# First loads asked for a stage ahead, modulation's weights in six loads, and row turning placed differently, in a two-layer diffusion trunk

## What is computed

```python
for i in range(DEPTH):                                  # 2 layers
    mod_l = split_cols(silu(c) @ w_mod[i] + b_mod[i])   # shift, scale, gate, twice
    mod_c = split_cols(silu(c_ctx) @ w_mod[i] + b_mod[i])
    a = modulate(rmsnorm(h, norm1_g[i]), ...)
    o = gla_mixer(...) if i == 0 else diff_mixer(...)   # mixer, ends in "@ w_out"
    h = h + gate * o
    f = modulate(rmsnorm(h, norm2_g[i]), ...)
    h = h + gate * peer_ffn(f, peer_wq[i], peer_subkeys[i], peer_u[i], peer_v[i])
return rmsnorm(h_lat, final_g)

def peer_ffn(h, wq, subkeys, u, v):
    q = (x @ wq).reshape(C, 8, 2, 128)                  # product keys
    s = einsum('chzd,zkd->chzk', q, subkeys)            # top 16 of 128, twice
    ...                                                 # top 16 of 256 pairs, softmax g
    act = gelu(einsum('cd,chkd->chk', x, u[idx]))       # rows of u, 16384 experts
    return einsum('chk,chkd->cd', g * act, v[idx])
```

## Time and profile before

| | us |
|---|---|
| median of 3 runs | 5217.56 (5213.93 to 5222.57) |
| the profiled execution | 5214.52 |
| its span | 5212.7 |

### The profile page before, as it was taken

The page is one execution under the profiler, slowest core; times in us unless marked ns, Lnnn a source line. Parts: engine busy times, 40 slices in busy tenths (PEclk is TensorE's granted clock), DMA queues, the critical chain, the costliest instruction groups (busy, mean ns, idle before and its releaser), DMA issues. The chain is left out here.

```text
span 5212.7 us, 54609 instructions
## 1 busy us (share of the span) xinstructions
PE 4361.0 (84%) x18847; PEld 2971.3 (57%) x18847; DVE 3454.1 (66%) x7226; ACT 1212.6 (23%) x2191; POOL 1825.8 (35%) x1652
## 2 busy tenths in 40 slices
PE   5799985793887799999999957886737777999997
PEld 4476764483555466666666625553433435666665
DVE  2256665468988877776777745675588775666665
ACT  0223321110343311111111112331212332222222
POOL 0021112022666655554555500000126774343441
PEclk9899978897999899999999979997868889999999
DMA  7577764612899999999999946667318999999995
GB/s 251 188 226 210 224 191 137 223 62 94 328 374 346 332 374 359 356 358 343 369 356 359 350 129 187 193 167 203 125 65 313 339 336 359 356 355 357 356 358 196
DMA packets 514294, 1407.95 MB, mean 270 GB/s; under 512 B 45661, under 2 KB 128605, under 8 KB 509183
## 3 DMA queue, kind: packets, MB, share of 16 engines
q1 hardware_dynamic: 329726, 733.60, 43.3%
q0 software_dynamic: 184320, 671.17, 34.0%
HBM read 1226.33 MB, written 178.26 MB: 269 GB/s over the span
## 5 line engine op out<-in xcount | busy, mean ns | idle before, releaser
L1623 POOL DMA_INDIRECT expert_rows<-u_rows,peer_arena x640 | 893.1, 1395 | 1311.3 <-DVE expert_rows L1897 1049.2
L1668 PE MATMUL ps<-part_arena,peer_part_arena 128*128 128x384 f32 (+1 forms) x4096 | 1034.7, 335 | 29.5 <-DVE peer_part_arena L1940 27.6
L1897 DVE SCALAR_TENSOR_TENSOR expert_rows<-expert_rows,mixer_in 128x1024 f32<-128x1024 f32 x640 | 759.9, 1220 | 125.0 <-DMA expert_rows<-u_rows,peer_arena 121.8
L1640 PE MATMUL ps<-expert_rows,peer_arena 128*128 128x512 f32 x1024 | 540.3, 680 | 329.8 <-DVE peer_arena L1905 327.5
L1630 POOL DMA_INDIRECT expert_rows<-in_peer_v,peer_arena x640 | 729.4, 1140 | 195.1 <-issue 186.0
L1668 PEld LDWEIGHTS ps<-part_arena,peer_part_arena 128*128 128x128 f32 x4096 | 698.4, 189 | 92.4 <-issue 77.6
L1677 PE MATMUL ps<-best,peer_arena 128*128 128x512 f32 x1540 | 685.3, 592 | 0.0
L1668 PE MATMUL ps<-mixer_in_parts,peer_part_arena 128*128 128x384 f32 (+1 forms) x2048 | 632.9, 309 | 0.0
L1640 PEld LDWEIGHTS ps<-expert_rows,peer_arena 128*128 128x128 f32 x1024 | 212.4, 217 | 602.4 <-issue 311.7
L1924 DVE SCALAR_TENSOR_TENSOR peer_arena<-expert_rows,peer_arena 128x1024 f32<-128x1024 f32 x381 | 489.4, 1285 | 30.5 <-DVE peer_arena L1924 2.3
L1450 POOL TENSOR_TENSOR part_arena<-peer_arena,part_arena 128x1024 fp32r<-128x1024 f32 x32 | 76.4, 2390 | 1077.8 <-ACT part_arena L1427 1077.8
(11 more groups left out here) (250 smaller groups left out, 6212.9 us busy)
## 6 DMA issues: line engine op xcount, KB each, us to landing
peer_arena<-in_peer_u SPq DMA_DIRECT2D x256, 512.0 KB
best<-in_peer_v SPq DMA_DIRECT2D x154, 512.0 KB
mixer_arena<-in_peer_u SPq DMA_DIRECT2D x296, 256.0 KB, 7.5
u_rows<-mixer_arena SPq DMA_DIRECT2D x148, 512.0 KB, 6.3
hidden<-in_peer_u SPq DMA_DIRECT2D x216, 256.0 KB, 6.3
u_rows<-hidden SPq DMA_DIRECT2D x108, 512.0 KB, 4.8
gates<-peer_arena SPq DMA_DIRECT2D x20, 2048.0 KB
peer_arena<-in_peer_v SPq DMA_DIRECT2D x52, 512.0 KB
```

What stands on the lines that cost most here:

```text
L1623: pool.indirect_dma_start(u_ring[:, k % U_SLOTS, :], None, u_table, bass.IndirectOffsetOnAxis(u_index[s][:, m:m + 1], 0)).then_inc(u_row_i ...
L1640: mm = pe.matmul(ps[:, 2 + half, :], diag[m % V_SLOTS], v_ring[:, m % V_SLOTS, half * 512:half * 512 + 512], start=m == 0, stop=m == PAIRS ...
L1668: mm = pe.matmul(ps[:, 6, 0:dense_tok], left[j % len(left)][:, c, :], right[:, c, :], start=at == 0, stop=at == len(todo) - 1)
L1897: dve.scalar_tensor_tensor(out=rows, in0=rows, scalar=1.0, in1=B.x[:, :, rows_at + s * P:rows_at + s * P + P], op0=ALU.mult, op1=ALU.mult, ...
```

## The change

1. Each mixer, project_out and product_keys has its first loads in a function `ahead`. The norm ahead of gla, attention and product_keys calls it at its beginning; gla and attention call project_out's on SyncE between their last heads, when the region that the weights go to is free. Their semaphores are kept (`B.kept`) and not cleared between the layers; the clears are worked out after all stages are made.
2. project_out has four weight slots instead of two, filled ahead; the loops of TensorE (project_out) and SyncE (product_keys) are written out.
3. Modulation has a buffer for all 16 tiles and asks for them in six loads (1, 1, 2, 4, 4, 4 tiles) at once, ahead of hidden, gains and identity, whose wait is now the stage's last step on SyncE.
4. Turning units: modulation 10 to 4, beginning of gla 6 to 12, project_out 0 14 to 16, beginning of attention 8 to 4, project_out 1 10 to 12. In gla the first four are turned one after each log gate, and SyncE's loads of head 1's weights stand after the sixth and the ninth `follow`. In attention the four come after VectorE's part of the prologue, and SyncE waits for the prologue's last unit and loads head 2's weights before the first `follow`.

```diff
-TURNED_EARLY = (10, 14)
-TURNED_LATE = 10
+TURN_MOD, TURN_GLA, TURN_ATT, TURN_OUT = 4, 12, 4, (16, 12)
+OUT_SLOTS = 4
...
+        B.start_loads = [(B.h, a["hidden"]), (small[:, 0:5 * C], a["gains"]), (B.ident[:, :], a["ident"])]
+        stages = [make(modulation)]
         for layer, segs in ((0, (CTX, LAT)), (1, (LAT,))):
+            project = make(project_out, a["gla_w_out"] if layer == 0 else a["diff_w_out"], segs[0][0], layer, segs)
+            mixer = make(gla if layer == 0 else attention, project["ahead"])
+            keys = make(product_keys, layer, segs)
+            stages += [make(norm, layer, B.gains[:, layer], 0, 1, (CTX, LAT), 0, mixer["ahead"]),
+                       mixer, project,
+                       make(norm, layer, B.gains[:, 2 + layer], 3, 4, segs, SPARSE_TILES[layer], keys["ahead"]),
+                       keys, make(peer, layer, segs)]
...
         @block.sync
         def _(sp):
-            sp.dma_start(B.h[:, :, :], a["hidden"]).then_inc(start_in, 16)
-            sp.dma_start(small[:, 0:5 * C], a["gains"]).then_inc(start_in, 16)
-            sp.dma_start(B.ident[:, :], a["ident"]).then_inc(start_in, 16)
-            sp.wait_ge(start_in, 48)
             run(sp, "sync")
...
 def modulation(B):
-    M = 4
-    loads = 2 * C // M
+    SIZES = (1, 1, 2, 4, 4, 4)
...
     def sync(sp):
         sp.dma_start(raw, B.a["cond"]).then_inc(cond_in, 16)
         sp.dma_start(B.mod_bias, B.a["b_mod"]).then_inc(cond_in, 16)
-        for n in range(2):
-            tiles.load(sp, n, n % 2)
+        for n, m in enumerate(SIZES):
+            at = slice(FIRST[n], FIRST[n] + m)
+            sp.dma_start(w[:, at].rearrange("p m c n -> p m (c n)"), B.a["w_mod"][at].rearrange("m p c n -> p m (c n)")
+                         ).then_inc(w_in[n], 16)
+        for to, at in B.start_loads:
+            sp.dma_start(to, at).then_inc(start_in, 16)
         turner.begin(sp)
...
     def tensor(pe):
-        pe.sem_inc(tiles.used, 2)
         pe.wait_ge(cond_ready, 1)
-        for n in range(loads):
-            tiles.multiply(pe, n, n % 2, n * M)
+        for m in range(2 * C):
+            if m in FIRST:
+                pe.wait_ge(w_in[FIRST.index(m)], 16)
+            for c in range(C):
+                mm = pe.matmul(out[:, m, :], w[:, m, c, :], B.cond[:, c, :], start=c == 0, stop=c == C - 1)
+        mm.then_inc(summed, 1)
...
+    def sync(sp):
+        if ahead:
+            ahead(sp)
...
     def sync(sp):
         turner.begin(sp)
         for m in range(2):
             mod.load(sp, m, m)
-        for n in range(BEFORE):
+        for n in range(6):
             turner.follow(sp, n)
         sp.wait_ge(u_mm, LAST_QKG + 1)
-        weights(1)
+        weights(sp, 1)
+        for n in range(6, 9):
+            turner.follow(sp, n)
         sp.wait_ge(u_mm, NU)
-        v_weights(1)
+        v_weights(sp, 1)
+        for n in range(9, BEFORE):
+            turner.follow(sp, n)
...
+            if h + 2 <= H:
+                sp.wait_ge(u_mm, NU * (h + 2))
             if h + 2 < H:
-                sp.wait_ge(u_mm, NU * (h + 2))
-                v_weights(h + 2)
+                v_weights(sp, h + 2)
+            if h + 2 == H:
+                for n in range(OUT_SLOTS):
+                    project_ahead(sp, n)
...
             if UNITS[u][0] == Z:
                 log_gates(0, 0, u)
-        for n in range(BEFORE):
+                turner.turn(dve, place(0, u) - 1)
+        for n in range(NZ, BEFORE):
             turner.turn(dve, n)
         heads(dve, head)
...
     def sync(sp):
         turner.begin(sp)
+        sp.wait_ge(u_mm, NP)
+        weights(sp, 2)
         for n in range(BEFORE):
             turner.follow(sp, n)
-        sp.wait_ge(u_mm, NP)
-        weights(2, 0)
...
+        prologue(unit)
         for n in range(BEFORE):
             turner.turn(dve, n)
-        prologue(unit)
         heads(dve, head)
```

205 lines of the change are left out of this document (108 added, 97 removed).

## The result

The changed kernel takes 5135.04 us (median of 4 runs, 5133.48 to 5138.93) against 5215.75 (4 runs, 5213.3 to 5222.57) of the kernel before: a ratio of 0.9844, 95% interval 0.9827 to 0.9861, faster by 1.6%. The forecast was 5139. The profiled execution has a span of 5134.5 us, 78.2 less than before.

The account below looks back on a forecast made before the run. Outside the TensorE-bound peer stages, the prediction took transfers, filled by turning units, as the main limit. Terms -40 - 8 + 6 - 9.5 - 33 + 6 = -78.5 took 5217.6 to 5139 us, range 5112 to 5172.

Parts of the forecast that it names:

- Modulation, -40: Modulation: four units instead of ten and six loads at once end it at 65 us; -40, between -33 and -45.
- gla, -8: Beginning of gla: loads ahead save 17.5 us, twelve units make VectorE late by 9; -8 remains.
- The bounds, +5 to -24: gla's beginning: +5 if holds leave the queue empty for 13 us, -24 if all twelve units fit under TensorE.
- The two holds: gla's beginning: stores of units 6 and 9 wait behind SyncE's waits for TensorE's twelfth and last unit; bound +5.
- project_out, +6 and +6: Both project_out stages, full of transfers: two units more, four weights fewer; +6 each, between +1 and +10.
- product_keys, -9.5: Both product_keys: first loads, 4.9 and 4.6 us, become hidden in the norm ahead; -9.5, between -6 and -10.
- attention, -33: Beginning of attention: the head begins at +60 instead of +88.9, and TensorE is a projection ahead; -33, between -27 and -38.
- Peer stages, 0: Peer stages: TensorE is busy throughout with transfers hidden under it, and the change leaves them alone; 0.
- (1): Rival: units are cheaper beside TensorE, gla's beginning hides all twelve and gains 24 instead of 8; 5123, chance 0.17.
- (2): Rival: moved units and SyncE's waits cost more, in gla, modulation, project_out and attention; 30 us more, 5169, chance 0.21.
- (3): Rival: loads ahead in gla, product_keys and attention are not early in effect; 36 us lost, 5175, chance 0.04.
- (4): Rival: TensorE's clock stays at 1.2 GHz from modulation through gla's beginning; 106 us more, 5245, chance 0.03.

Follow-up runs that it names:

- hid_first: Changed kernel with hidden, gains and identity asked for ahead of modulation's six weight loads, without a wait between; 5144.2 us.
- mod10: Changed kernel with layer 0's units placed as before, ten in modulation and six at gla's beginning; 5157.2 us.
- g_early: Changed kernel with gla's first two units turned on VectorE before the first log gate; 5135.3 us.
- a_early: Changed kernel with two of attention's four units turned and stored ahead of VectorE's part of the prologue and SyncE's wait for TensorE's fifth unit; 5124.2 us.
- no_ahead: Changed kernel with the first loads of gla, attention and product_keys asked for at the stage's own beginning, not in the norm ahead; 5177.1 us.
- heads5: Changed kernel with eight units fewer in the project_out stages (12 and 8) and five units per attention head instead of four; 5089.3 us.
- no_out_ahead: Changed kernel with each project_out's four first weights asked for at its own beginning, not in gla and attention; 5151.1 us.
- the repetition: The changed kernel measured again with no edit, in a later group of runs; 5138.9 us.
- g_early2: g_early with SyncE's loads of head 1's weights moved behind the ninth and twelfth unit's stores; 5123.3 us.

## Why the prediction was right, point by point

**The time.** 5139 against 5135.0, in a range of 5112 to 5172. The forecast's case held; the errors of its terms are +5 us in gla, -3 in project_out 1 and -3 in the norms. That they cancel to less than 1 us is luck.

**Modulation, -40: -40.4.** End foreseen at 65, measured 64.64, with the 256 records in one stretch of 54.75 us. The sum of bytes carried it: the window shows 324 GB/s, where 317 was taken. TensorE's end, at 60.25, was close behind, as the upper bound said, and hid_first shows the margin, 4 us. The forecast gave no split; mod10 gives it: nine tenths are the units.

**gla, -8: -2.9 in the first pair of profiles, none in the second.** The first product came at once, as foreseen (-17.5). The first k_d transpose slipped to +108.6, foreseen +107.5 (17.5 less the slip of 9 is 8.5, which the prediction wrote as 8). The step that failed is the sentence that put "all of head 0" behind it, as if it took as long as before: the way from that transpose to the forward part took 49.3 us instead of 44.5 (14.6 us of slip at the forward part, of which 9.8 stood at the transpose). The windows show where the 4.8 us are. Each cuts this way in two at the same instruction, 31 or 32 records behind its beginning and 203 ahead of its end, after first, then before:

```profile
208.62:218.20 9.58, 9.58 (x31) 8.37 (x32) 3.78 (x8) 4.93 (x8) 0.00 (x0) 0.50 1.05 298
218.30:257.80 39.50, 37.31 (x203) 30.30 (x201) 16.18 (x33) 15.55 (x26) 0.00 (x0) 0.89 1.02 313
```
```profile
257.60:262.60 5.00, 5.00 (x32) 4.62 (x32) 1.38 (x4) 4.52 (x7) 0.00 (x0) 1.00 0.36 81
262.60:302.00 39.40, 37.41 (x203) 30.39 (x201) 15.71 (x32) 15.96 (x28) 0.00 (x0) 0.89 1.04 319
```

Behind its wait of 17.21 us TensorE does in 9.58 us what took 5.00 before: its granted clock is 0.50, the lower level, 1.2 GHz, instead of 1.00. The remaining 203 records take the same time in both, with one wait of 2.2 us for a tile of w_mod against 2.0, so the full queue costs nothing more here. The prediction priced VectorE's delay, and not what TensorE's rest does to the work behind it. The other runs bear out that it goes with the rest: in the seven other profiles with this wait (16.8 to 18.9 us; g_early, a_early, no_ahead, hid_first, heads5, no_out_ahead and the repetition) the 16 records on w_mod right behind the transpose take 3.41 or 3.42 us, as here, and where the wait is missing (before, mod10, g_early2) 1.84 or 1.85. Taking the rest away didn't give the 4.8 us back, though: g_early2 needs 49.4 us for the same part, with two other stretches of lower clock inside it (0.57 from 193.7 to 197.7, 0.68 from 207.9 to 218.5) that no run here explains. The bounds, +5 to -24, held the term. The two holds that the bound of +5 priced (SyncE's waits between the stores) cost nothing in the changed kernel, and 15 us as soon as the units came earlier (g_early).

**project_out, +6 and +6: +6.6 and +3.0.** The mechanism was right (full queue, two units more, four weights less; no_out_ahead puts the weights at 12.2 us for the two, 15.2 foreseen). The size of the second was off by the rate that the profile of before happened to show, 293 GB/s against 310 after: 88 us at 310 are 27.3 MB, which at 293 would have been 93 us, +7.

**product_keys, -9.5: -9.6** with the norms ahead of them, -10.5 without. As foreseen.

**attention, -33: -32.3.** The head begins at +59.3 (foreseen +60), behind the wait of 17.44 us that was named; a_early shows the mechanism by taking it away.

**Peer stages, 0:** +1.8 and -1.2, inside what they move by themselves. The norms' 3 us less was not foreseen, and no run here explains it.

**The rivals.** (1), all twelve units hidden: false, with them gla's forward part begins 22 us behind TensorE's own time (mod10). (2), everything dearer: gla's slip was 14.6 and not 22, modulation not 33. (3), loads not early in effect: false, they are worth 38 to 42 (no_ahead), 36 foreseen. (4), the lower clock from modulation through gla's beginning: false, the granted clock was 1.00 in modulation and 0.87 over gla's first 158 us, where the lower level throughout would be 0.50; 9.6 us of it in a row were at that level. The Trainium skill's figure for the part of a transfer that grows with its size (DMA: Bandwidth & Descriptors, Anatomy of one DMA, a fit of transfers issued from GpSimd; bytes over 436 GB/s) gives, as an estimate, 58 us for twelve units; the runs disagree as the trace of before did, with 6.0 us per unit in modulation (mod10) and 6.2 in the project_out stages (heads5).

## What to carry to other kernels

Where several stages are full of transfers, put nothing on a stage that is already at a share of 1 while another has 0.8: eight units moved so were worth more than half of the whole change. Where side work makes TensorE rest, look at the clock of the work behind the rest and not only at the length of the rest: 17.21 us of waiting were followed here by 4.6 us more for the same instructions. When the issuing engine waits in its own stream, look at what it would hold up if the rest came earlier; a gap that closes in one place opens at the next wait in that stream, and the two have to be moved together. An idle stretch of an engine at the beginning of a stage, ahead of the first value it needs, is the cheapest place for side work, if its data can already be there.

## What the runs showed of the hardware that was not expected

- **A full queue has no fixed rate.** The same stage's code at a share of 0.99 to 1.02 moved 293 GB/s in one profile and 317 in another. project_out 1 with twelve units took 93.7 us at 293 and 86.3 at 317 (windows of mod10 and of g_early; the product is 27.3 MB in both), project_out 0 with sixteen 122.1 and 113.8:

```profile
3542.00:3635.00 93.00, 65.58 (x128) 27.64 (x128) 35.22 (x56) 0.00 (x0) 0.00 (x0) 0.83 1.02 293
```
```profile
3521.00:3607.00 86.00, 63.57 (x128) 26.86 (x128) 34.98 (x56) 0.00 (x0) 0.00 (x0) 0.86 1.01 317
```

  A term that rests on one window's rate carries 4% either way. What sets the rate no run here shows.
- **Pauses go with longer work of TensorE itself.** The 256 records of project_out 0 were busy for 89.19 us with pauses between them (granted clock 0.90, a mean of stretches at the upper level, 2.4 GHz, and some at the lower, 1.2 GHz) and for 84.70 without (0.97, nearly all at the upper): 4.5 us on top of the pauses themselves, which no sum of busy times shows. The clearest case is in gla: behind a rest of 17.21 us the same instructions took 9.58 us at 0.50 that took 5.00 at 1.00 in the kernel before.
